# First modulation by channel halves, the first three input tiles in two passes over the channels

## The reference

```python
c_act = jax.nn.silu(c)
for l in range(DEPTH):
    ada = c_act @ w_ada[l] + b_ada[l]
    sh1, sc1, gt1, sh2, sc2, gt2 = [t[:, None, :] for t in jnp.split(ada, 6, axis=-1)]
    u = x * (1.0 + sc1) + sh1
    y = mixer(u, cos, sin, w_in[l], ...)
    x = layer_norm(DN_ALPHA * x + (1.0 + gt1) * y, ln_mix_g[l], ln_mix_b[l])
    ...
```

## Time and profile before

| | |
|---|---|
| median of three runs | 1811.62 us |
| span of the profiled execution | 1813.6 us (the profile gives nothing around it) |
| TensorE busy | 1755.5 us, 97% |
| VectorE busy | 1275.5 us, 70% |
| ScalarE busy | 891.5 us, 49% |
| HBM read | 343.69 MB, mean 190 GB/s over the span |
| DMA in the first slice of 45 us | 300 GB/s |

### The profile page before, as it was taken

How to read it: one execution, slowest core, us unless ns; L and a number is a source line. 1 busy time by engine, 2 the same in 40 slices (tenths; PEclk the granted TensorE clock), 3 DMA queues, 4 the chain that set the end, 5 groups by cost and what they waited for, 6 DMA issues and landing times.

```text
span 1813.6 us, 26735 instructions
## 1 busy us (share of the span) xinstructions
PE 1755.5 (97%) x9254; PEld 1450.9 (80%) x9254; DVE 1275.5 (70%) x1973; ACT 891.5 (49%) x1530; POOL 57.3 (3%) x111
## 2 busy tenths in 40 slices
PE   8999999998999999998999999999999999999998
PEld 3776778996766779987998977788889989778886
DVE  5788887667788885568557987655555588865555
ACT  1456434443455444444556664544455667544443
POOL 0000010000000000002000000000000000000000
PEclk9999999999999999999999999999999999999999
DMA  8866568774866566663665444555646645345553
GB/s 300 267 213 218 162 216 301 253 230 133 264 220 209 185 210 209 209 190 110 210 215 156 131 142 141 174 185 184 190 153 200 215 131 160 117 155 182 184 186 126
DMA packets 216040, 346.29 MB, mean 191 GB/s; under 512 B 19611, under 2 KB 113353, under 8 KB 215673
## 3 DMA queue, kind: packets, MB, share of 16 engines
q1 hardware_dynamic: 213448, 338.89, 58.3%
q0 software_dynamic: 1632, 5.39, 1.0%
q10 hardware_dynamic: 850, 0.54, 0.1%
HBM read 343.69 MB, written 1.07 MB: 190 GB/s over the span
## 4 chain that ended last, share of the span: by engine, by line
issue 79%; PE 12%; DVE 4%; DVEq 1%; POOLq 1%; POOL 1%; ACT 0%; DMA 0%; SPq 0%; ACTq 0%
PE acc L150 2%; PE acc L148 2%; PE acc L149 2%; PE prod L223 1%; PE prod L225 1%; PE prod L224 1%; DVE w_lo L134 1%; DVEq L937 1%; PE prod L148 1%; DVE proj L938 1%; PE prod L150 1%; PE prod L149 1%; PE turn L262 0%; DVE x_res L938 0%; DVE x_res L936 0%
## 5 line engine op out<-in xcount | busy, mean ns | idle before, releaser
L134 DVE TENSOR_TENSOR w_lo<-w_raw,w_hi 128x1024 fp32r<-128x1024 f32 (+2 forms) x584 | 643.7, 1122 | 308.6 <-ACT w_hi L128 302.9
L128 ACT CAST w_hi<-w_raw 128x1024 fp32r<-128x1024 f32 (+2 forms) x584 | 557.9, 968 | 406.6 <-PE acc L150 186.3
L148 PE MATMUL prod<-w_hi,hT_hi 128*128 128x512 f32 (+2 forms) x880 | 319.8, 363 | 4.7 <-ACT proj_b L1949 3.6
L150 PE MATMUL prod<-w_hi,hT_lo 128*128 128x512 f32 (+2 forms) x880 | 313.0, 356 | 0.0
L149 PE MATMUL prod<-w_lo,hT_hi 128*128 128x512 f32 (+2 forms) x880 | 312.3, 355 | 0.0
L148 PEld LDWEIGHTS prod<-w_hi,hT_hi 128*128 128x128 f32 x880 | 166.3, 189 | 25.0 <-DVE gates L2202 5.9
L150 PEld LDWEIGHTS prod<-w_hi,hT_lo 128*128 128x128 f32 x880 | 166.3, 189 | 15.4
L149 PEld LDWEIGHTS prod<-w_lo,hT_hi 128*128 128x128 f32 x880 | 166.8, 189 | 14.6
L223 PE MATMUL prod<-uT_hi,w_hi 128*128 128x256 f32 x448 | 127.1, 284 | 1.6 <-DVE w_lo L134 1.1
L148 PE MATMUL prod<-w_hi,uT_hi 128*128 128x512 f32 x304 | 124.6, 410 | 2.7 <-DVE uT_lo L301 1.3
L224 PE MATMUL prod<-uT_lo,w_hi 128*128 128x256 f32 x448 | 126.4, 282 | 0.0
(11 more groups left out here) (349 smaller groups left out, 2836.6 us busy)
## 6 DMA issues: line engine op xcount, KB each, us to landing
w_raw<-in_w_in_dram SPq DMA_DIRECT2D x72, 512.0 KB, 3.8
ada_raw<-in_w_ada_dram SPq DMA_DIRECT2D x68, 512.0 KB, 6.7
w_raw<-in_w_in_dram SPq DMA_DIRECT2D x192, 172.0 KB, 2.4
w_raw<-in_w_up_dram SPq DMA_DIRECT2D x64, 512.0 KB, 4.4
w_raw<-in_w_down_dram SPq DMA_DIRECT2D x64, 512.0 KB, 4.5
w_raw<-in_w_gate_dram SPq DMA_DIRECT2D x128, 192.0 KB, 2.6
w_raw<-in_w_ffn_gate_dram SPq DMA_DIRECT2D x88, 256.0 KB, 3.6
w_raw<-in_w_ffn_up_dram SPq DMA_DIRECT2D x88, 256.0 KB, 4.3
```

Of the source, the lines that this page charges most:

```text
L128: act.copy(self.hi[:, s, 0:cols], self.raw[:, s, 0:cols]).then_inc(self.hi_done, 1)
L134: dve.tensor_tensor(self.lo[:, s, 0:cols], self.raw[:, s, 0:cols], self.hi[:, s, 0:cols].bitcast(F32), ALU.subtract).then_inc(self.lo_done, 1)
L148: pe.matmul(out, a_hi, w_hi, start=first and c == 0, stop=False)
L150: mm = pe.matmul(out, a_lo, w_hi, start=False, stop=last and c == chunks - 1)
```

## The change

Shift and scale of layer 0 are now made for channels 0 to 511 first and for 512 to 1023 later. Each of the 16 chunks holds two of the eight values of k and 512 columns instead of one and 1024, 512 KB as before. TensorE makes them as `mod_rows` does, on 32 columns of `c_wide` (`first_rows`), ScalarE copies the 97 rows (`first_part_take`), and TensorE multiplies them with two columns of `pick`, which sums the strips and puts the result with channels on partitions (`first_columns`). x is loaded first and turned right away; the modulation is then applied to the turned x, by ScalarE directly to `uT_hi` (`first_u_hi`), by VectorE to `vT`, from which `uT_lo` is taken. The first three tiles (a, g, q) are computed in `prod`, `acc[0:2]` and `acc[2:4]`, all of them over the first half of the channels and then over the second (`SPLIT_IN`). The tables of taps differ by layer now.

```diff
+IN_TAPS = (((0, 0, 4, 4), (4, 3, 3, 3), (0, 0, 3, 3)), ((5, 5, 3, 3), (3, 3, 3, 3), (0, 0, 3, 2)))
+PAIR_TAPS = (((6, 5, 4, 7, 6), (5, 4, 3, 7, 5), (5, 4, 3, 6, 5), (5, 4, 3, 6, 4)),
...
+SPLIT_IN = [(t, g) for h in range(2) for t in range(3) for g in (2 * h, 2 * h + 1)]
...
-        FIRST = [(v, k) for k in range(6) for v in (1, 0)] + [(1, 6), (1, 7), (0, 6), (0, 7)]
+        FIRST = [(h, v, 2 * j) for h in range(2) for v in (1, 0) for j in range(4)]
...
SyncE
+            load_constants(sp)
+            for i in range(8):
+                first_chunks(i)
+                if i == 1:
+                    sp.dma_start(pick[:, :], dr["pick"]).then_inc(pick_in, 16)
                     bias_rows.load(sp)
...
+                    for i, (t, g) in enumerate(SPLIT_IN):
+                        if i == 4:
+                            for n in range(8, 12):
+                                first_chunks(n)
+                        if i == 6:
+                            for n in range(12, 16):
+                                first_chunks(n)
+                        weights(layer(l, i, G1), w_in, g * KG * P, slice(IN_ORDER[t] * NT, (IN_ORDER[t] + 1) * NT))
+                        if i == 9:
...
+                            half_bias(0)
+                            sp.wait_ge(first_used, 2 * DC)
+                            half_rows(0)
...
ScalarE
+            for n in range(4):
+                T.take(act, layer(0, F_U + n, F_ALL), xT[:, 4 * (n % 2):4 * (n % 2) + 4, n // 2 * P:(n // 2 + 1) * P],
+                       view=lambda s: s.rearrange("p (c t) -> p c t", c=4))
             bias_rows.copy(act, prod[0])
+            act.wait_ge(part_zero, 1)
+            first_part_take(0)
+            first_part_take(1)
...
+                    split(layer(l, 4, G1), 2)
+                    first_part_take(2)
+                    first_part_take(3)
+                    split(layer(l, 6, G1), 1)
+                    for c in range(4, DC):
+                        first_u_hi(c)
+                    split(layer(l, 7, G1), 1)
...
VectorE
+                    first_columns(0)
+                    first_u(0)
                     split(layer(l, 0, G1), 1)
+                    first_u_lo(0)
+                    first_u(2)
                     split(layer(l, 1, G1), 1)
+                    first_u_lo(2)
+                    split(layer(l, 2, G1), 4)
+                    first_columns(1)
+                    first_u(4)
+                    first_u_lo(4)
+                    split(layer(l, 6, G1), 1)
+                    first_u(6)
+                    first_u_lo(6)
+                    split(layer(l, 7, G1), 1)
...
TensorE
+            for n in range(4):
+                rows_turn(layer(0, F_U + n, F_ALL), x_res[:, n // 2, :], 4 * (n % 2))
+            bias_rows.multiply(pe, prod[0])
...
+                    for k in range(k0, k0 + 2):
+                        c = k % 4 * 32
+                        mm = pe.matmul(T.bank[v][c:c + 32, :], c_wide[:, k, 0:32], first_raw[i][:, k % 2 * NT:(k % 2 + 1) * NT],
+                                       start=k < 4, stop=k >= 4)
...
+                    for c in range(4):
+                        mm = pe.matmul(T.bank[v][:, 2 * c:2 * c + 2], first_part[v][:, c * P:(c + 1) * P], pick[:, 0:2], start=True, stop=True)
...
+                    for i in range(1, 5):
+                        split_group(i)
+                    first_rows(1, 1)
+                    first_rows(1, 0)
+                    split_group(5, lambda: first_columns(1))
+                    for i in range(6, 12):
+                        if i < 8:
+                            pe.wait_ge(first_lo, i - 3)
+                        split_group(i)
+                    gated_turn(0)
+                    conv_w_turns()
+                    mod_rows(0)
...
```

## The result

| | before | change |
|---|---|---|
| median | 1811.82 us (16 runs) | 1815.45 us (16 runs) |
| ratio | | 1.0016 [1.0009, 1.0023] |
| span of the profiled execution | 1813.6 us | 1814.6 us |
| time less span, median | 1.80 us | 1.96 us |

The change is slower by 0.16%, 2.9 us by the ratio (1.6 to 4.2). The forecast was 2.3 us faster, and 1815.45 lies outside the range of 1804.5 to 1814.8.

The account below looks back on a forecast made before the run. The prediction took the start, without projection work until 39.2 us, and VectorE's pace in the pairs as bounds. A 5.5 us gain at tile 3 less 3.2 for late taps gave 2.3 shorter: 1809.3 us, eight-in-ten range 1804.5 to 1814.8.

Parts of the forecast that it names:

- The base of the sum: Whole kernel: profiled span 1813.6 us, 2.0 above the median 1811.62; that distance was left as it is.
- The first half of the modulation: Start: eighth chunk landed at 21.4 us, first projection matmul at 27.9 against 39.2, bounds 25 and 31.
- The clock: Behind the start: TensorE at the low level for 5 us, until 34.2, slowing the first groups.
- the early release of the forecast: First groups: the low clock level ends early, after 3.5 us as seen near 187 us; 5 us was taken.
- the other case: First groups: the low clock level lasts 15.1 us, as at the start of before.
- The groups, second rows and gap: Input groups: 1.8 us wait before group 6, tile 3 ending at 87.9 us against 93.4, gain 5.5.
- The taps: Head pairs: seven convolution taps left over where VectorE sets the pace, 3.2 us back, about 2 in pair 0.
- A wait ahead of them that was put at nothing: Before the pairs: VectorE, followed from group 14 on, arrives within 0.2 us of TensorE's pace as before.
- That the taps cost nothing: Rival, head pairs: VectorE has room for the late taps, so the 5.5 us gain stays, 1806.1 us; chance 0.24.
- The array that is slow up to 43 us: Rival, groups 1 to 4 and gap before group 6: low clock costs 6.1 us more, 1815.4 us; chance 0.13.
- The first half was ahead: Start: first-half chunks land first; the opposing rival had first matmul at 31 us or later, 1812.8 us, chance 0.13.

Follow-up runs that it names:

- the cuts: Kernels shortened to layer 0, or both layers, of the first block, then x written out; layer 0 alone: 444.78 us before, 446.68 with the change.
- before_l1_again: Repeat of the kernel before shortened to layer 0 of the first block, otherwise unchanged: 444.67 us.
- before_late_taps: Whole kernel before with the change's pair tap table for layer 0, 27 instead of 33 taps behind the input groups: 1816.29 us, ratio 1.0022.
- before_block1_l2: The kernel before without the second block, both layers of the first block kept, then x written out: 845.86 us.
- before_copy: The whole kernel before, unchanged, run again for a second trace: 1812.48 us, ratio 1.0002.
- after_l1_again: Repeat of the changed kernel shortened to layer 0 of the first block: 446.06 us.
- The early turns: The change with the convolution's first turns before group 11 and 33 taps behind the input groups: 1810.88 and 1810.3 us whole, 442.35 with layer 0 only.
- before_block1_l1: The kernel before shortened to layer 0 of the first block, then x written out, first measurement: 444.78 us.
- before_warm_l1: The kernel before, layer 0 of the first block only, with 13 instead of 6 dummy matmuls at TensorE's start: 445.94 us.
- early_awake_l1: Layer-0 change with earlier convolution turns, plus dummy matmuls: 13 instead of 6 at the start, others around the first columns and before group 6: 444.57 us.

## Why the prediction was wrong, by its own steps

**The base of the sum: wrong, the main fault.** The prediction noted that the profiled span stood 2.0 us above the median and left "that distance as it is". The distance was part of what it meant to gain. The trace had caught the slow start of before: four records of row products took 3.78 us up to 23 us and 1.98 us from 24.09, and none of them waited for a chunk, so the array at the low level set that start. By their times 4 of 22 executions of the cuts had this start. In the one quick execution of these cuts that was traced (before_l1_again) the array is quick from 11.4 us on and waits 0.67 us for a chunk at 26.58, so the transfers set the start, and by this the lead at the end of the fourth input tile is 3 us smaller. That the other 17 started alike is read from their times. Of the whole kernel unchanged both traces have the slow start; before_late_taps (36.74 us) and before_block1_l2 (36.35), which are the same kernel up to there, have quicker ones. The change has no such gain to make, since it waits for transfers whichever level the array has: its first matmul stood at 26.1 to 27.5 in five traces, with the first rise of the clock anywhere from 4.2 to 20.4 us.

**The first half of the modulation: right in its steps, 1.8 us too long.** The last chunk of the half was used at 21.55 (21.4 forecast), GpSimd's load came at 16.56 (16). The 1.9 us between 21.4 and 23.3 us of the forecast, for eight records of row products at the low level, no run shows: behind the last landing four records ran, in 1.05 us, and the granted clock was 1.00 there (20.0 to 25.3 us). The pick products took 1.95 us and not 3.3, and the first projection matmul stood at 26.13 (27.9).

**The clock: right in kind.** It was low behind the start, for 6.8 us up to 32.1, at 0.50, and the first projection matmul stood in that stretch (forecast: 5 us, up to 34.2). The low stretch ended while the groups ran, after 6.8 us in three traces of the change and after 3.4 in two (the early release of the forecast; the other case was the 15.1 us of before). What the forecast lacked is that in the kernel before the first rise came anywhere from 4.6 us (before_l1_again) to 23.3 (before_copy), behind the same instructions.

**The groups, second rows and gap: right.** 1.82 us before group 6, ended by VectorE's low half (1.8 forecast); the end of tile 3, the fourth input tile, at 86.15 (87.9), the difference being that of the start. The gain in the profiled executions was 7.3 us, 5.5 forecast.

**The taps: right. A wait ahead of them that was put at nothing: wrong, the second fault.** Pair 0's turn waited 1.94 us for the probabilities (2 forecast), pair 1's 1.52 in after_l1_again (more than 0.77 forecast). In the pairs the change loses 2.0, 0.8 and 0.4 us to the quick before, together the 3.2 of the forecast; the table alone cost 2.9 in the cut and 4.0 in the whole kernel. But 1.7 us more are lost before the pairs. The sentence that VectorE "arrives within 0.2 us of TensorE's pace as before" failed at the first turn of `glu_rows`, where TensorE waits 1.56 us. The count of taps was compared, and not the time that VectorE has for them: it idled for late high parts before 83.87 us, and then worked without a pause up to the turn. The early turns take back 3.8 us (whole) and 4.3 (cut), and both waits shrink to 0.3 us or less; how much of the 1.7 us belongs to the taps' late start and how much to the late weight transfer is not separated.

**The sum with both put right**: 3.4 us ahead at the end of the fourth tile (5.5 forecast), 3.2 lost in the pairs (3.2), 1.7 lost at `glu_rows` (nothing): 1.5 us slower. These are the two traces of the cut, whose spans differ by 1.6; the cuts' medians say 1.9 and 1.4. In one respect the cut is not the whole kernel: the cut before is 0.5 us quicker from its first projection matmul to the end of the fourth tile (53.8 against 54.25 us). The whole kernel is slower by 2.9 (1.6 to 4.2). 0.16 us of it lie around the span; whether the rest of the difference is more than its uncertainty is open, and the longer wait at the join is a candidate that is not shown. The price of single falls of the clock, like the one in pair 0, is open too.

**The rivals.** That the taps cost nothing is refuted by four kernels. The array that is slow up to 43 us named 1815.4, next to the result, for a reason that did not occur: the low stretch ended at 32.1 and not 43. The first half was ahead. That the kernel before is quicker than its profile was no rival, and should have been one.

## What to carry to other kernels

Compare the profiled span, with the time around it, with the median before working out a gain: where it is longer by as much as the gain, ask which wait of the trace a usual execution doesn't have, above all a stretch at the low level of the clock. Where a change moves work to an engine's earlier time, follow that engine's queue up to the next place where another waits for it, with its idle time, and not only its count of work. And cut a kernel behind the stage in question: with one layer the executions agreed within 1.4 us and showed two groups, which the whole kernel's spread of 6 us hid.

## What the runs showed of the hardware

- The same instructions of before, from 7.8 us on, ran at the low level for 3 to 4 us (before_late_taps, before_l1_again), 9 (before_block1_l2) or 15 (before, before_copy, before_block1_l1). By its time the first, profiled execution was slow in three of four cuts of before, the other executions in one of 18.
- The profile's granted clock begins with the first rise: for the start of before it says 1.00, while four records took 3.78 us and, at the high level, 1.98. There the durations tell, and the clock column doesn't.
- With 13 dummy matmuls at the start the clock rose at 7.5 us (before_warm_l1) and 5.3 (early_awake_l1), and both kernels were slower, by 1.2 and 2.2 us. In the first TensorE waited 2.33 us for a chunk up to 26.57, and the clock fell behind it (28.0 to 31.4 us).
- Sixteen small records (128 by 128 weights, two columns each) took 1.95 us at the high level (after, at 22.53 us), 0.12 each.
